# A decoder layer on one core: the first norm writes where the expert products read, and the first group's weights are loaded ahead

## What is computed

```python
h = x @ w_in                       # q, k, v, pooling input, gates
o = rms_norm(diff_attention(q, k, v), subln_g) * (1 - lam_init)
attn_branch = o @ w_attn_proj
pool_branch = (pooled @ pool_w * pool_scale) @ w_pool_proj
merged = g_attn * attn_branch + g_pool * pool_branch
y = layer_norm(ALPHA * x + merged @ w_out, ln1_g, ln1_b)
q = y @ w_q                        # per head: two halves against 128 keys
idx, gate = top16 of the 16 x 16 best sums, softmax
act = gelu(sum_d u[idx] * y)       # the products
ffn = sum_e gate * act * v[idx]
out = layer_norm(ALPHA * y + ffn, ln2_g, ln2_b)
```

## Time and profile before

| | |
|---|---|
| median of 3 runs | 3466.81 us (3465.33 to 3469.37) |
| the profiled execution | 3465.91 us |
| its span, first to last instruction | 3464.1 us |
| granted TensorE clock, mean | 0.949 of full |
| busy: PE, DVE, POOL, ACT | 2852.0, 2473.6, 1224.9, 1184.4 us |
| DMA moved | 1251.28 MB, mean 361 GB/s |
| start of the first gather, of the first product | 343.75 us, 370.59 us |

### The profile page before, as it was taken

The page is one execution under the profiler, slowest core; times in us unless marked ns, Lnnn a source line. Parts: engine busy times, 40 slices in busy tenths (PEclk is TensorE's granted clock), DMA queues, the critical chain, the costliest instruction groups (busy, mean ns, idle before and its releaser), DMA issues.

```text
span 3464.1 us, 30304 instructions
## 1 busy us (share of the span) xinstructions
PE 2852.0 (82%) x8384; PEld 1464.5 (42%) x8384; DVE 2473.6 (71%) x5985; ACT 1184.4 (34%) x3487; POOL 1224.9 (35%) x1184
## 2 busy tenths in 40 slices
PE   9998799888997789888987989867877777777776
PEld 7775455444443345344444444323333222222222
DVE  2213678786588877889788877888788676667664
ACT  2201345444222233344554532223332333333332
POOL 0000233333233344334343443444444443444442
PEclk9999899999998899998999999979999999999999
DMA  6442899898999999999999899999999999999997
GB/s 213 165 164 80 320 349 357 323 334 313 353 391 395 414 420 420 419 352 343 355 352 364 330 382 420 402 381 421 420 420 420 416 421 417 418 418 414 419 417 314
DMA packets 206953, 1251.28 MB, mean 361 GB/s; under 512 B 23872, under 2 KB 37184, under 8 KB 75328
## 3 DMA queue, kind: packets, MB, share of 16 engines
q0 software_dynamic: 147456, 1073.81, 77.4%
q1 hardware_dynamic: 58320, 175.40, 13.6%
q10 hardware_dynamic: 1008, 0.14, 0.0%
HBM read 1231.96 MB, written 17.30 MB: 361 GB/s over the span
## 4 chain that ended last, share of the span: by engine, by line
PE 42%; DMA 31%; DVE 15%; issue 6%; ACT 4%; POOL 2%; SPq 1%; POOLq 0%; DVEq 0%
DMA ring<-uv,idx 28%; PE r_o L1517 16%; PE w_ps L1315 13%; DVE ring L1252 6%; DVE z_e L1204 3%; PE w_ps L1432 2%; PE w_ps L1363 2%; PE r_o L1487 1%; PE w_ps L1455 1%; POOL ring L648 1%; DMA s<-s_scr 1%; DMA wc<-w_branch 1%; ACT e L725 1%; PE w_ps L1487 1%; ACT diag L839 1%
## 5 line engine op out<-in xcount | busy, mean ns | idle before, releaser
L1517 PE MATMUL r_o<-ring,diag 128*128 128x512 f32 x2952 | 1476.7, 634 | 457.7 <-ACT diag L839 445.0
L648 POOL DMA_INDIRECT ring<-uv,idx x1024 | 1145.1, 1118 | 1924.5 <-PE r_o L1517 1383.2
L1252 DVE CUSTOM_DVE_ANT_0 ring<-ring,ytok 128x1024 f32<-128x1024 f32 x1024 | 1250.5, 1222 | 434.3 <-DMA ring<-uv,idx 418.0
L1517 PEld LDWEIGHTS r_o<-ring,diag 128*128 128x128 f32 x2952 | 551.4, 198 | 1198.7 <-ACT diag L839 658.7
L1315 PE MATMUL w_ps<-x,w 128*128 128x384 f32 (+1 forms) x2112 | 662.1, 461 | 13.0 <-DMA w<-w_in 7.0
L826 ACT ACTIVATE gel<-dot 128x2 f32<-128x2 f32 x512 | 103.8, 203 | 1547.7 <-DVE dot L1252 1538.7
L1315 PEld LDWEIGHTS w_ps<-x,w 128*128 128x128 f32 x2112 | 404.0, 195 | 242.7 <-issue 68.2
L1204 DVE SCALAR_TENSOR_TENSOR z_e<-ring,coef,z_e 128x1024 f32<-128x1024 f32 x286 | 366.0, 1280 | 6.0 <-ACT coef L830 6.0
L839 ACT ACTIVATE diag<-ident,coef 128x128 f32<-128x128 f32 x738 | 264.1, 387 | 9.7 <-PE r_o L1517 9.7
L830 ACT ACTIVATE coef<-gel,gate 128x1 f32<-128x1 f32 x1024 | 246.0, 287 | 16.7
L1487 PE MATMUL w_ps<-yT,wq 128*128 128x384 f32 x512 | 202.4, 511 | 0.1
(11 more groups left out here) (189 smaller groups left out, 2337.6 us busy)
## 6 DMA issues: line engine op xcount, KB each, us to landing
w<-w_in SPq DMA_DIRECT2D x132, 512.0 KB, 3.5
wq<-wq SPq DMA_DIRECT2D x48, 512.0 KB
wc<-w_branch SPq DMA_DIRECT2D x24, 768.0 KB
ring<-uv,idx POOLq DMA_INDIRECT x1024
wo<-w_out SPq DMA_DIRECT2D x24, 512.0 KB, 15.4
xs<-x SPq DMA_DIRECT2D x8, 512.0 KB
y_scr<-zn SPq DMA_DIRECT2D x8, 512.0 KB, 7.6
ytok<-y_scr SPq DMA_DIRECT2D x8, 512.0 KB
```

Of the source, the lines that this page charges most:

```text
L648: nc.gpsimd.indirect_dma_start(out=ring[t % RING][:], out_offset=None, in_=a["uv"], in_offset=bass.IndirectOffsetOnAxis(ap=idx[:, slot:slo ...
L1252: nc.vector.tensor_tensor_reduce(ring[r][:, 0:D], ring[r][:, 0:D], ytok[n % 2][:], 1.0, 0.0, ALU.mult, ALU.add, dot[:, slot:slot + 1]).the ...
L1517: ins = nc.tensor.matmul(o_ps[n % 2][half][:], diag[(u - 1) % DIAGS][:], ring[t % RING][:, D + half * HALF:D + (half + 1) * HALF], start=s ...
```

## The change

Four things. (1) `w_branch` of group 0 has eight buffers, one per block, at 24 to 72 KB; the loads are spread in SP's order over the attention steps, six slots apart, with the search keys behind the last. What of group 1 used this space (pool_w, bias, saved keys and values) is now issued after the last branch step. (2) The norm of group 0 writes into `ytok` itself, tile 2 into `ytok[0]`, tile 5 into `ytok[1]`; tiles 6 and 7 stay in buffers of their own (`zn2`), and the products read them there. Only tiles 3 and 4 go by DRAM. The wait of a third residual falls away, and so does POOL's wait for the writes of group 0. (3) Query blocks 2 and 3 of group 0 have own buffers, loaded with blocks 0 and 1; blocks 4 and 5 may be asked for two queries earlier. (4) The eight pieces of `x` of groups 1 and 2 share one semaphore, waited for once.

```diff
+PARKED = (T0S[1] + 1, T0S[1] + 2)
-    wc = [[at(f"wc{g}{r}", ((74, 80), (95, 36), (0, 6))[g][r], [P, CA + CP, P]) for r in range(2)] for g in range(NG)]
+    wc = [[at(f"wc0{n}", 24 + 6 * n, [P, CA + CP, P]) for n in range(DC)]]
+    wc += [[at(f"wc{g}{r}", ((95, 36), (0, 6))[g - 1][r], [P, CA + CP, P]) for r in range(2)] for g in range(1, NG)]
-    zn = [[at(f"zn{g}{u}", (157, 40, 77)[g] + 4 * u, [P, D]) for u in range(2)] for g in range(NG)]
+    ytok = [at(f"ytok{u}", 181 + 4 * u, [P, D]) for u in range(2)]
+    zn = [ytok, [ytok[0]] + [at(f"zn1{u}", 40 + 4 * u, [P, D]) for u in range(2)],
+          [ytok[1]] + [at(f"zn2{u}", 77 + 4 * u, [P, D]) for u in range(2)]]
+    wq_early = [at(f"wq_early{r}", 65 + 4 * r, [P, D]) for r in range(2)]
+    def y_of(n):
+        if n < T0S[2]:
+            return ytok[n % 2]
+        return zn[2][n - T0S[2]]
...
 # SP, tokens(g)
-            elif g == NG - 1:
+            elif g == 1:
+                yield branch_at(0, DC) + 2
+                sp.wait_ge(merge_done, DC)
+            else:
                 yield norm_at(1, GTS[1]) + 15
-                sp.wait_ge(y1_out, 16 * KTS[g - 1])
+                sp.wait_ge(y1_out, 16 * len(PARKED))
             sp.dma_start(pw_raw[g][:], a["pool_w"]).then_inc(pw_in[g], 16)
...
 # SP, keys_back(g), and values_back(g) likewise
-                yield step_at(g, GTS[g] * h - 3) if h > 1 else (0, step_at(0, 2 * GTS[0]), score_at(1, RH) + 1)[g]
+                yield step_at(g, GTS[g] * h - 3) if h > 1 else (0, branch_at(0, DC) + 3, score_at(1, RH) + 1)[g]
+                if h == 0 and g == 1:
+                    sp.wait_ge(merge_done, DC)
...
         def load_query(g, hp):
+            if g == 0 and hp in (2, 3):
+                return
             if hp >= 2:
-                sp.wait_ge(q_unit, k - 1)
+                sp.wait_ge(q_unit, HP * g + hp - (3 if g == 0 and hp in (4, 5) else 1))
...
         def rest(g):
             if g == 0:
-                yield EARLY - 1
-                load_branch(0, 0)
-                load_branch(0, 1)
+                for n in range(DC):
+                    yield EARLY - 1 + 6 * n
+                    if n == 0:
+                        sp.wait_ge(lam_step, 2)
+                    sp.dma_start(wc[0][n][:], a["w_branch"][n]).then_inc(c0_in[n], 16)
                 load_keys(0)
...
-            for n in range(2, DC):
+            for n in range(2, DC) if g else ():
                 yield branch_at(g, n - 1)
                 load_branch(g, n)
...
             load_query(g, 1)
+            if g == 0:
+                for r in range(2):
+                    sp.dma_start(wq_early[r][:], a["wq"][2 + r]).then_inc(wq_early_in[r], 16)
...
-        def first_norm_out(g):
-            for n in range(GTS[g]):
-                t = T0S[g] + n
-                yield norm_at(g, n + 1) + 11
+        def first_norm_out():
+            for i, t in enumerate(PARKED):
+                n = t - T0S[1]
+                yield norm_at(1, n + 1) + 11
                 sp.wait_ge(y1_ready, t + 1)
-                sp.dma_start(y_scr[t], zn[g][n % 2][:]).then_inc(y1_out, 16)
+                sp.dma_start(y_scr[i], zn[1][n][:]).then_inc(y1_out, 16)
...
-        tokens_in(0)
-            if n + 1 < TT and slot % SLOTS == (116 if n + 1 in T0S else 20):
+            if n + 1 in PARKED and slot % SLOTS == 20:
                 tokens_in(n + 1)
...
 # POOL, ahead of the first gather
-        pool.wait_ge(y1_out, 16 * GTS[0])
 # DVE, transposed, residuals, products
+                if g == 1 and k == 0:
+                    dve.wait_ge(q_unit, 4)
-                        if n >= 2:
-                            dve.wait_ge(y1_out, 16 * (t - 1))
-                            dve.wait_ge(tr_ready, 2 * (t - 1))
-            dve.wait_ge(y_in[n % 2], 16 * (n // 2 + 1))
+            if n in PARKED:
+                dve.wait_ge(y_in[PARKED.index(n)], 16)
+            else:
+                dve.wait_ge(y1_ready, n + 1)
-            nc.vector.tensor_tensor_reduce(ring[r][:, 0:D], ring[r][:, 0:D], ytok[n % 2][:], 1.0, 0.0, ALU.mult,
+            nc.vector.tensor_tensor_reduce(ring[r][:, 0:D], ring[r][:, 0:D], y_of(n)[:], 1.0, 0.0, ALU.mult,
 # PE, units(g)
-                    if i == 0:
-                        pe.wait_ge(x_in[g][c], 16)
+                    if i == 0 and g == 0:
+                        pe.wait_ge(x_in[c], 16)
+                    elif i == 0 and c == 0:
+                        pe.wait_ge(x_all_in[g - 1], 16 * DC)
```

More of the change, by code:

```diff
@@ L290, in build @@
     coef = at("coef", 180.5, [P, SLOTS])
-    ytok = [at(f"ytok{u}", 181 + 4 * u, [P, D]) for u in range(2)]
     z = at("z_e", 189, [P, D])
@@ L358, in build @@
         [sem(f"bias_in{g}") for g in range(NG)], sem("small_in"), [sem(f"pw_in{g}") for g in range(NG)])
-    x_in = [[sem(f"x_in{g}{c}") for c in range(DC)] for g in range(NG)]
+    x_in, x_all_in = [sem(f"x_in{c}") for c in range(DC)], [sem(f"x_all_in{g}") for g in range(1, NG)]
     w_in = [[sem(f"w_in{g}{k}") for k in range(RAWS)] for g in range(NG)]
@@ L371, in build @@
     p_step, p_done, pm_unit, pm_scaled = sem("p_step"), sem("p_done"), sem("pm_unit"), sem("pm_scaled")
-    c_in, c_unit, gated, merge_done = [sem("c_in0"), sem("c_in1")], sem("c_unit"), sem("gated"), sem("merge_done")
+    c0_in, c_in = [sem(f"c0_in{n}") for n in range(DC)], [sem("c_in0"), sem("c_in1")]
+    c_unit, gated, merge_done = sem("c_unit"), sem("gated"), sem("merge_done")
     wo_in, gb1_in = [sem(f"wo_in{c}") for c in range(DC)], sem("gb1_in")
@@ L394, in build, with branch_weights, query_weights, query_count @@
     block = ctx.enter_context(nc.Block())
+    def y_of(n):
+        if n < T0S[2]:
+            return ytok[n % 2]
+        return zn[2][n - T0S[2]]
+    def branch_weights(g, n):
+        return wc[0][n] if g == 0 else wc[g][n % 2]
+    def query_weights(g, hp):
+        return wq_early[hp - 2] if g == 0 and hp in (2, 3) else wq[g][hp % 2]
+    def query_count(g, hp):
+        return 16 * (hp // 2 + (0 if hp >= 4 else 1)) if g == 0 else 16 * (HP // 2 * g + hp // 2)
     @block.sync
@@ L458, in values_back @@
             for h in range(H):
-                yield step_at(g, GTS[g] * (h - 1)) + 8 if h > 1 else (0, step_at(0, 2 * GTS[0]), score_at(1, RH) + 1)[g]
-                if h == 0 and g == NG - 1:
+                yield step_at(g, GTS[g] * (h - 1)) + 8 if h > 1 else (0, branch_at(0, DC) + 3, score_at(1, RH) + 1)[g]
+                if h == 0 and g == 1:
+                    sp.wait_ge(merge_done, DC)
+                elif h == 0:
                     sp.wait_ge(q_unit, HP * g)
@@ L546, in stage @@
         def stage(g):
-            parts = [units(g), tokens(g), rest(g), first_norm_out(g), scoring(g)]
+            parts = [units(g), tokens(g), rest(g), scoring(g)]
             if g < NG - 1:
@@ L551, in stage @@
                 parts += [keys_back(g), values_back(g)]
+            if g == 1:
+                parts.append(first_norm_out())
             return merged(*parts)
@@ L562, in tokens_in @@
         def tokens_in(n):
-            if n >= 2:
-                sp.wait_ge(joined, 2 * n - 2)
-            sp.wait_ge(y1_out, 16 * (n + 1))
-            sp.dma_start(ytok[n % 2][:], y_scr[n]).then_inc(y_in[n % 2], 16)
+            i = PARKED.index(n)
+            sp.wait_ge(joined, 2 * n - 2)
+            sp.wait_ge(y1_out, 16 * (i + 1))
+            sp.dma_start(ytok[n % 2][:], y_scr[i]).then_inc(y_in[i], 16)
         def store(n):
@@ L1190, in join @@
                 return
-            nc.vector.scalar_tensor_tensor(z[:, cols], ytok[n % 2][:, cols], ALPHA, o_ps[n % 2][half][:], ALU.mult,
+            nc.vector.scalar_tensor_tensor(z[:, cols], y_of(n)[:, cols], ALPHA, o_ps[n % 2][half][:], ALU.mult,
                                            ALU.add).then_inc(joined, 1)
@@ L1195, in lay_base @@
             dve.wait_ge(yn_ready, n + 1)
-            nc.vector.tensor_scalar(z[:], ytok[n % 2][:], ALPHA, None, ALU.mult).then_inc(z_based, 1)
+            nc.vector.tensor_scalar(z[:], y_of(n)[:], ALPHA, None, ALU.mult).then_inc(z_based, 1)
         def add_row(t):
@@ L1431, in branches @@
                         pe.wait_ge(o_ready, STEP0[g] + GTS[g] * (j + 1))
-                    ins = nc.tensor.matmul(bank, wc[g][c % 2][:, j, :], o_all[g][:, j, :], start=j == 0, stop=j == CA - 1)
+                    ins = nc.tensor.matmul(bank, branch_weights(g, n)[:, j, :], o_all[g][:, j, :], start=j == 0, stop=j == CA - 1)
                 ins.then_inc(c_unit, 1)
@@ L1436, in branches @@
                     yield branch_at(g, n) + (CA + j) * BRANCH_LEN[g] // (CA + CP)
-                    ins = nc.tensor.matmul(bank, wc[g][c % 2][:, CA + j, :], pm[g][:, j, :], start=j == 0, stop=j == CP - 1)
+                    ins = nc.tensor.matmul(bank, branch_weights(g, n)[:, CA + j, :], pm[g][:, j, :], start=j == 0, stop=j == CP - 1)
                 ins.then_inc(c_unit, 1)
@@ L1481, in queries @@
                     pe.wait_ge(k_in, 16 * (g + 1))
```

(5 more changed lines are left out.)

34 lines of the change are left out of this document (18 added, 16 removed).

## The result

The changed kernel takes 3433.64 us (median of 4 runs, 3431.99 to 3434.56) against 3468.09 us (4 runs, 3465.33 to 3469.40) for the kernel before on the same chip: ratio 0.9901, 95% interval 0.9884 to 0.9918, or 34.5 us less. The forecast was 3431. The profiled execution took 3433.76 us, 32.2 under the profiled one of before.

The account below looks back on a forecast made before the run. PE was taken to set the pace from 400 to 900 us, DMA from 2500 us on. Gains of 9.0 + 5.7 + 11.9 + 8.1 = 34.7 us off 3465.9 gave 3431 us, range 3421 to 3447.

Parts of the forecast that it names:

- Step 1: Loads from 70 us on: 3.15 MB less before the awaited `w_in` block, stall gone, 9.0 us gained (4.5 to 9.0).
- The slack of the `w_in` blocks: Heads between 87 and 190 us: a block has 5.1 us to spare, so a 2.45 us branch block fits in.
- Step 2: Wait for the third `w_branch` block, landed at 214.14 us, goes whole: 5.7 us gained (5.2 to 5.7).
- Step 3: Group 1's loads after the last branch step land 4 us before the first pooling product: price nothing (0 to -3).
- Step 4: Before the first slots: the first product no longer waits for the read of `ytok[0]`, 11.9 us gained (8 to 14).
- Query blocks: Blocks 2 to 5 of group 0: price nothing; without the 2.1 us cover, up to 4.2 us in play.
- Step 5: Six writes and six reads of 0.524 MB fall away; they count in full-DMA stretches: 8.1 us gained (0 to 10.0).
- the wait on q_unit 4: Added wait whose event is over long before it is reached: priced at nothing.
- The rival of the clock: PE's granted clock or a later wait eats more of the gain: 3446 us or more, chance 0.06.
- that bytes don't count: Last stage paced by latency of gather, sum and next gather: 26.6 us gained, 3439 us, chance 0.14.
- that part of the start comes back: Narrow fits at the burst, pooling product and first product fail together by half, 10.5 us: 3442 us, chance 0.11.
- the slower one: Between 87 and 190 us branch blocks delay `w_in` blocks and starve the units: 3475 us, chance 0.04.

Follow-up runs that it names:

- double_branch: Changed kernel with branch blocks 2 to 7 each loaded a second time, into a buffer nobody uses: 3432.39 us (ratio 0.9883).
- y_two: Kernel before with only tiles 0 and 1 normed into the token buffers, tiles 2 to 7 still by DRAM: 3454.87 us (ratio 0.9963).
- y_only: Kernel before with all of the first norm's part alone (only tiles 3 and 4 by DRAM), branch and query blocks as before: 3443.76 us (ratio 0.9936).
- two_query: Changed kernel without the two further query buffers, blocks 2 to 5 asked for one query ahead: 3432.70 us (ratio 0.9895).
- extra_reads: Changed kernel with 16 further plain reads of 0.524 MB after slot 780, into a buffer nobody uses: 3453.96 us (ratio 0.9954).
- branch_only: Kernel before with only the branch weights' part and the one semaphore for `x`: 3452.77 us (ratio 0.9958).

## Why the prediction was right, and where it was not

The sum was 34.7; the medians differ by 34.5, the profiled executions by 32.2. The second can be taken apart: 7.7 + 5.7 + 11.9 + 10.6 - 3.9 = 32.0. Against the sum that is 1.3 less at the burst, 2.5 more from the bytes and 3.9 lost to a wait that was priced at nothing. That these errors cancel in part, and that the medians lie 2.3 us further apart than the two profiled executions, for which no step has a reason, is luck; the three large steps are not.

- **Step 1, the burst: 7.7 instead of 9.0.** The mechanism is right, the size is off, since 1.20 us of the wait stay. The step divided 5.50 MB by the mean rate of the larger burst, 321 GB/s. This burst didn't have that rate: its 5.50 MB took from 73.3 to 91.7 us, 300 GB/s. (Both rates count only the blocks of the burst; with all else that moved the stretches had 377 GB/s before and 330 now.) DMA ran at 265 GB/s and a share of 0.78 to 0.88 until 85 us, so it wasn't full, and at 409 to 427 after it, while SP issued nearly without a break from 76.86 to 84.83 us: 4.43 us for the eight parts of `x`, 2.40 for four `w_in` blocks. That the issuing set the pace there is argued from this; no run varied it.
- **The slack of the `w_in` blocks** (5.1 us against 2.45 per branch block) held, and holds for twice the load (double_branch). By the prediction's own numbers the last block with the search keys (5.7 us) did not fit; no wait was seen there either.
- **Step 2, the third branch block: 5.70, as worked out.** SP's issue of `xs` came at 248.17 before and at 234.75 now, 13.4 earlier, of which 7.7 stood before the branch steps.
- **Step 3, what is issued behind the last branch step: nothing, right.** The pooling product comes 266.35 - 252.93 = 13.4 earlier, with no wait.
- **Step 4, the first product: 11.9, right**, in the changed kernel and alone (11.3 in y_two, 11.5 in y_only). The rows were there before DVE asked. Of the wait for query block 5, 2.38 of 4.20 are left; as PE's own work ends at 344.71 + 0.92 and the diagonals come at 350.60, they are covered. **Query blocks: nothing, right** (two_query).
- **Step 5, the bytes: 10.6 instead of 8.1**, as 21.7 to 32.3 in the changed kernel and 12.5 to 23.1 in y_only up to slot 800. That transfers before 900 us are free held (y_two), and the reads of tiles 5 to 7 are seen one by one at their slots, 0.9 to 1.3 us each against 1.25 (and 1.3 in extra_reads). What was missed lies between slots 192 and 256, a step of 5.0 to 5.7. In the kernel before, SP's timeline and DVE's wait are these:

```profile
1063.74 0.33 SPq L529 DMA_DIRECT2D y_scr<-zn  x1
...
1085.87 4.11 SPq L415 DMA_DIRECT2D x<-xT  x8
1090.02 9.40 SPq L408 DMA_DIRECT2D w<-w_in  x3
1099.52 2.86 SPq L560 DMA_DIRECT2D s<-s_scr  x1
...
1133.22 0.49 DVE L1102 MAX8 top<-s 128x8 f32<-128x128 f32 x2 [3.49 <-DMA s<-s_scr]
```

  and in the changed kernel:

```profile
1062.43 4.77 SPq L437 DMA_DIRECT2D x<-xT  x8
1067.24 2.38 SPq L430 DMA_DIRECT2D w<-w_in  x3
1069.72 2.83 SPq L596 DMA_DIRECT2D s<-s_scr  x1
```

  The scores of a head were asked for at 1099.52, needed at 1129.7 and there at 1133.2; now they are asked for 29.8 us earlier at a lead of 22, and DVE doesn't wait. y_two and branch_only, which keep the write of tile 2, have this wait too (2.81 and 1.80 us), y_only has not. So a transfer less in front of SP's line seems to have been worth a wait behind it, not only its 1.25 us. That it is the write of tile 2 and not another of the part's transfers is argued from the order of the issues; no run took that one alone. The 2.54 us of the third residual belong to the same place and can't be told apart from it.
  By the Trainium skill (Perfetto Trace Analysis, Roofline) a core that works alone may pass the 358 GB/s of its share, up to about 435 GB/s; 418 over 925 us and 427 over 4 us in this trace agree, and no run here shows the case of two cores.
- **What the prediction did not have: the loss of 3.9 us.** Part 5 put down "the wait on q_unit 4" at nothing, "their events are over long before". That is the step that failed. Its event was over, and the wait still cost 3.7 to 4.1 us in the profiles and 2.6 to 5.5 by the medians: it moved one of DVE's later instructions by 0.37 us, PE stood 0.37 us longer behind that, and the clock fell. The prediction also named a shrinking lead between 400 and 2250 us as a sign that it is wrong, and the lead shrank, from 25.6 to 21.8 between 450 and 550 us. By its own sign this part of it is wrong, and so is "no DMA wait of L1315 at 90 us", where 1.20 us stayed. The rival of the clock had the right kind of mechanism ("no row ties such a change to this one") and too high a price. Against it stand the 2.5 us that step 5 gave more, and so the total fits better than its parts.
- **The rivals:** that bytes don't count (3439) is refuted by extra_reads; that part of the start comes back happened by 1.3 us at the burst, not by 10.5; the slower one is refuted by double_branch; and each part alone moves the time, which refutes that the change does nothing.

## What to carry to other kernels

Take a transfer's worth at the place where it is waited for: the token read paid 11.9 us at one slot, three transfers in the PE-bound stretch nothing that can be seen, those in the DMA-bound one 1.25 us each, and one that stood in front of others in a queue some 5, if the reading of step 5 is right. A wait that is always over when it is reached is not free by that: here it shifted an instruction by 0.37 us, and by way of PE's clock 4 us were lost, so leave out waits that nothing needs (the one here exists only for a buffer that gained nothing). A test that puts load on a queue must be checked in the trace for where the load went: the 16 reads went out in three groups, and the block that was to leave the burst stood behind the one that was waited for. Before a smaller burst is priced by the mean rate of a larger one, look whether the issuing queue or the bytes set that rate.

## What the runs showed of the hardware

- A standstill of PE of 1.67 to 1.69 us near slot 38 left the granted clock at its upper level, 2.4 GHz; after one of 2.04 to 2.06 us at the same place, after the same work, it fell to 1.2 GHz for a part of the stretch from 470 to 475 us of the changed kernel (0.68 on the mean), and so in all eight kernels with the wait. The price was some 2 us, five times the 0.37 us that came first. Near slot 54 a standstill of 2.15 to 2.16 us left the clock up in the six kernels without the wait and was followed by its fall in the eight with it, so the length of the last standstill does not decide alone.
- The 0.37 us themselves: with the further wait some 47 us earlier in DVE's stream, DVE starts the copy later behind the same event, and a pause of 0.15 us before the instruction after it is gone. In the kernel before, that instruction reads so:

```profile
496.60 1.23 DVE L1252 CUSTOM_DVE_ANT_0 ring<-ring,ytok 128x1024 f32<-128x1024 f32 x1 [0.15 <-issue]
```

  In the changed kernel it follows the copy at once (471.18). It looks as if a pause that belongs to a place in the stream was moved from one instruction to the one before it; what makes the pause stays open (0.37 and 0.15 us are not the same size), and so does why the clock falls a second time, near slot 54.
